# A fused two-block decoder on one core: conditioning weights partly summed ahead of their matmul, and causal attention outputs with the values stationary

## The reference, cut to what matters

```
sh1, sc1, g1, sh2, sc2, g2 = split(silu_c @ ada_w[i] + ada_b[i], 6)       # and the same with silu(c_ctx)
h = rmsnorm(x, norm_mix[i]) * (1.0 + sc1) + sh1
x = x + g1 * attention(h);  x = x + g2 * conv_ffn(rmsnorm(x, norm_ffn[i]) * (1.0 + sc2) + sh2)
```

```
o_nsa = g0 * o_cmp + g1 * softmax(causal(q @ k_s.T)) @ v_s + g2 * softmax(causal(q @ k_w.T)) @ v_w
o_fox = softmax(causal(f_q @ f_k.T + decay)) @ f_v                        # 4 heads of 64
o_pool, o_conv = moving averages, short causal convolution
for i, o in enumerate((o_nsa, o_pool, o_conv, o_fox)):
    acc += sigmoid(merge[i]) * ((o * silu(gates[i])) @ w_branch[i])
x = x + acc @ w_out
```

## Time and profile before

| | |
|---|---|
| median of three runs | 1595.04 us (1594.56 to 1595.25) |
| the profiled execution | 1595.22 us |
| its span (first to last instruction) | 1593.4 us |
| granted TensorE clock, mean | 0.997 |
| PE busy | 1568.6 us, 98% |
| DVE / ACT / POOL busy | 936.4 / 750.5 / 543.3 us |
| layer 0 of block two starts about | 1094 us; layer 1 is the same pattern some 255 us later |

### The profile page before, as it was taken

One profiled execution on the slowest core, in us unless ns is written; L12 is line 12 of the kernel. 1 busy time (PEld: TensorE's weight loads), 2 busy tenths in 40 slices (PEclk: granted clock), 3 DMA queues, 4 the chain that ended last, 5 costly groups with the idle time before them and its releaser, 6 DMA issues.

```text
span 1593.4 us, 23097 instructions
## 1 busy us (share of the span) xinstructions
PE 1568.6 (98%) x9146; PEld 1303.4 (82%) x9146; DVE 936.4 (59%) x1441; ACT 750.5 (47%) x1360; POOL 543.3 (34%) x354
## 2 busy tenths in 40 slices
PE   8999999999999999999999999999999999999998
PEld 5778557778887888879768899989998889998887
DVE  4434485555575554342266888757876457968435
ACT  5324485444322433243375755445654445654444
POOL 2224243322211222212273111007424657623663
PEclk9999999999999999999999999999999999999999
DMA  9264500534174222364313754454534534633551
GB/s 393 94 246 187 212 30 9 204 135 157 63 268 184 80 81 73 124 207 164 123 37 113 267 192 172 162 190 170 183 133 161 199 143 171 215 133 132 185 211 54
DMA packets 52603, 249.17 MB, mean 156 GB/s; under 512 B 20624, under 2 KB 21008, under 8 KB 26256
## 3 DMA queue, kind: packets, MB, share of 16 engines
q1 hardware_dynamic: 43744, 243.90, 42.2%
q10 hardware_dynamic: 8752, 3.80, 1.0%
HBM read 246.63 MB, written 1.05 MB: 155 GB/s over the span
## 4 chain that ended last, share of the span: by engine, by line
PE 88%; DVE 5%; ACT 3%; issue 1%; DMA 1%; POOL 1%; SPq 0%; POOLq 0%; ACTq 0%; DVEq 0%
PE psq L554 16%; PE psq L555 16%; PE psq L556 16%; PE ps L554 7%; PE ps L556 7%; PE ps L555 7%; PE psq L970 3%; PE ps L568 1%; PE psq L971 1%; PE ps L970 1%; DMA RAW<-wstream 1%; ACT WHL L526 1%; PE psq L1365 1%; PE ps L1393 1%; PE psq L2298 1%
## 5 line engine op out<-in xcount | busy, mean ns | idle before, releaser
L536 DVE TENSOR_TENSOR WHL<-RAW,WHL 128x1024 fp32r<-128x1024 f32 (+3 forms) x264 | 324.9, 1254 | 290.1 <-ACT WHL L526 289.6
L536 POOL TENSOR_TENSOR WHL<-RAW,WHL 128x1024 fp32r<-128x1024 f32 (+2 forms) x116 | 304.5, 2627 | 504.6 <-ACT WHL L526 471.8
L526 ACT ACTIVATE WHL<-RAW 128x1024 fp32r<-128x1024 f32 (+2 forms) x380 | 361.4, 1002 | 196.1 <-DMA RAW<-wstream 98.6
L554 PE MATMUL psq<-NHL,WHL 128*128 128x256 f32 (+1 forms) x1072 | 353.8, 330 | 1.7 <-POOL WHL L536 0.7
L555 PE MATMUL psq<-NHL,WHL 128*128 128x256 f32 (+1 forms) x1072 | 349.0, 326 | 0.0
L556 PE MATMUL psq<-NHL,WHL 128*128 128x256 f32 (+1 forms) x1072 | 348.9, 325 | 0.0
L554 PEld LDWEIGHTS psq<-NHL,WHL 128*128 128x128 f32 x1072 | 205.2, 191 | 28.9 <-issue 7.5
L556 PEld LDWEIGHTS psq<-NHL,WHL 128*128 128x128 f32 x1072 | 205.3, 191 | 16.6
L555 PEld LDWEIGHTS psq<-NHL,WHL 128*128 128x128 f32 x1072 | 205.3, 191 | 15.4
L554 PE MATMUL psq<-WHL,NHL 128*128 128x512 f32 (+1 forms) x320 | 124.8, 390 | 1.7 <-DVE WHL L536 1.7
L556 PE MATMUL psq<-WHL,NHL 128*128 128x512 f32 (+1 forms) x320 | 123.3, 385 | 0.0
(11 more groups left out here) (389 smaller groups left out, 2975.6 us busy)
## 6 DMA issues: line engine op xcount, KB each, us to landing
RAW<-wstream SPq DMA_DIRECT2D x194, 1024.0 KB, 4.8
RAW<-wstream SPq DMA_DIRECT2D x32, 704.0 KB, 4.0
K<-first SPq DMA_DIRECT2D x4, 1024.0 KB, 17.2
RAW<-wstream SPq DMA_DIRECT2D x4, 800.0 KB, 4.3
X<-xin SPq DMA_DIRECT2D x2, 1024.0 KB, 6.1
V<-first SPq DMA_DIRECT2D x2, 1024.0 KB, 19.3
Q<-first SPq DMA_DIRECT2D x2, 1024.0 KB, 24.7
BR<-rpb ACTq DMA_DIRECT2D x8, 256.0 KB, 8.2
```

What stands on the lines that cost most here:

```text
L526: e.activation(WH[:, u % 3, a:z], RAW[:, v % 3, a:z], ACT.Copy).then_inc(w_hi, 1)
L536: e.tensor_tensor(WL[:, u % 3, a:z], RAW[:, v % 3, a:z], WH[:, u % 3, a:z].bitcast(F32), ALU.subtract).then_inc(w_lo_p if pool else w_lo_v, 1)
L554: e.matmul(o, lh, rh, start=start, stop=False)
```

## The change

**Conditioning.** In pass b=1 units 0, 1, 6 and 7 are no longer multiplied on PE: DVE adds each of them, times a column of CB, into two buffers of 128x2048 (one for c, one for c_ctx), units 0 and 1 ahead of the splits of projection units 1 and 2, units 6 and 7 behind the whole rotation loop. Units 2 to 5 stay on PE, two after projection unit 5 and two after 6. A joint matmul of both sums (8 matmuls) stands ahead of value unit 1, the turn ahead of value unit 2. Pass b=3 has its units 4 to 7 summed at MLP units 1, 3, 5, 7 in the same way, with the joint ahead of unit 8. In passes 5 and 6 the units only run closer together. A load behind a summed unit now waits for DVE's sum.

**Hybrid layers.** DVE multiplies the probabilities by the reciprocal (times the gate) in SBUF, ahead of their transposes (`dve_causal_scale`, nine TENSOR_TENSORs of 128x512 per layer), and the transposes wait for that in place of the exponential. The output matmul holds 64 columns of values stationary in either half of the array's columns, with 128 or 256 columns of probabilities moving, so that outputs arrive transposed, all in one PSUM bank; the selected, the window and the compressed attention add up there. `dve_causal_out`, `dve_cmp_out` and the transposes `pe_turn_nsa` and `pe_turn_fox` are gone. Fox's output times its gate runs on DVE after scale 4, its high part on ACT after exponential 5, the rest on DVE after scale 5; output matmul 2 waits for the first of them, since it reuses the bank.

**Heads and g2.** A weight split moves into the norm loop, ACT's copy of KF moves behind a split, and the first half of g2's matmuls is put ahead of the scores of job 0.

```diff
-UP_ADA = {("up", 0, 0): (0, 1, 2, 3), ("up", 0, 2): (4,), ("up", 0, 3): (5,), ("up", 0, 4): (6,), ("up", 0, 5): (7,)}
-QKV_ADA = {("qkv", 1, 4): (0, 1, 2), ("qkv", 1, 5): (3,)}
-JOINT_ADA = {("up", 0, HALF_FT + 1): (7,)}
-LATE_ADA = {("up", 1, 0): (0, 1, 2), ("up", 1, 1): (3,)}
+FIRST_ADA = {3: (0,), 4: (1,), 5: (2, 3), 6: (4, 5), 9: (6,), 10: (7,)}
+FIRST_SUMMED = {1: (0,), 2: (1,)}
+FIRST_ON_PE = {5: (2, 3), 6: (4, 5)}
+UP_ADA = {("up", 0, 0): (0, 1, 2, 3)}
+UP_SUMMED = {1: 4, 3: 5, 5: 6, 7: 7}
+QKV_ADA = {("qkv", 1, 4): (0, 1, 2, 3)}
+LATE_ADA = {("up", 1, 0): (0, 1, 2, 3)}
+SUMMED = {1: (0, 1, 6, 7), 3: (4, 5, 6, 7), 4: tuple(range(8))}
+JOINT_AT = {("qkv", 0, 9): 1, ("up", 0, 8): 3, ("up", 0, HALF_FT + 1): 4}
...
-            if v >= 3 and KEYS[v - 3][:2] == ("ada", 4):
-                e.wait_ge(ada_acc, KEYS[v - 3][2] + 1)
+            if v >= 3 and KEYS[v - 3] in ADA_ACC:
+                e.wait_ge(ada_acc, ADA_ACC[KEYS[v - 3]])
...
-        def dve_ada_step(e, k):
-            v = UNIT_OF["ada", 4, k]
+        def weight_sums(b):
+            if b == 1:
+                return [t.rearrange("p a n -> p (a n)") for t in (PP[:, 3:7, :], TMP[:, 4:8, :])]
+            return [WSUM[:, c, :] for c in range(1 if b == 4 else 2)]
+
+        def dve_ada_step(e, b, k):
+            v = UNIT_OF["ada", b, k]
+            sums = weight_sums(b)
+            at = ADA_ACC["ada", b, k] - len(sums)
             e.wait_ge(d_raw[v % 3], 16 * (v // 3 + 1))
-            if k == 0:
-                e.tensor_scalar(WSUM[:, :], RAW[:, v % 3, :], CB[:, k, 0:1], None, ALU.mult).then_inc(ada_acc, 1)
-                return
-            e.wait_ge(ada_acc, k)
-            e.scalar_tensor_tensor(out=WSUM[:, :], in0=RAW[:, v % 3, :], scalar=CB[:, k, 0:1], in1=WSUM[:, :],
-                                   op0=ALU.mult, op1=ALU.add).then_inc(ada_acc, 1)
-
-        def pe_ada_joint(e):
-            e.wait_ge(ada_par, 3)
-            e.wait_ge(ada_acc, 8)
-            for j in range(4):
-                mm = e.matmul(AB[32 * j:32 * j + 32, :], ONE.to_broadcast([P, 32]), WSUM[:, 512 * j:512 * j + 512],
-                              start=True, stop=True)
+            if b == 4 and k == 0:
+                e.wait_ge(gemm, product(("joint", 3)))
+            for c, t in enumerate(sums):
+                if k == SUMMED[b][0]:
+                    e.tensor_scalar(t, RAW[:, v % 3, :], CB[:, k, c:c + 1], None, ALU.mult).then_inc(ada_acc, 1)
+                    continue
+                e.wait_ge(ada_acc, at - len(sums) + c + 1)
+                e.scalar_tensor_tensor(out=t, in0=RAW[:, v % 3, :], scalar=CB[:, k, c:c + 1], in1=t,
+                                       op0=ALU.mult, op1=ALU.add).then_inc(ada_acc, 1)
+
+        CBF = CB[:, :, :].rearrange("p k n -> p (k n)")
+        ONE_AT = (CBF[:, 16:48], CBF[:, 15:47])
+
+        def pe_ada_joint(e, b):
+            if b == 4:
+                e.wait_ge(ada_par, 3)
+            e.wait_ge(ada_acc, ADA_ACC["ada", b, SUMMED[b][-1]])
+            for c, t in enumerate(weight_sums(b)):
+                for j in range(4):
+                    mm = e.matmul(AB[32 * j:32 * j + 32, :], ONE_AT[c], t[:, 512 * j:512 * j + 512], start=b == 4,
+                                  stop=b == 4 or c == 1)
             mm.then_inc(gemm, 1)
 
         def act_ada_row(e, b):
-            e.wait_ge(gemm, product(("ada", b, ada_units(b) - 1)))
+            e.wait_ge(gemm, product(("joint", b) if b in SUMMED else ("ada", b, ada_units(b) - 1)))
...
-                    for _ in range((0, 0, 0, 2, 2, 2, 1, 1)[i]):
-                        pe_ada(e, 1, next(late_ada))
+                    for k in FIRST_ON_PE.get(i, ()):
+                        pe_ada(e, 1, k)
             for i in range(4):
                 if l == 0 and i == 1:
+                    pe_ada_joint(e, 1)
+                if l == 0 and i == 2:
                     pe_ada_turn(e, 1)
                 pe_values(e, l, i)
...
+                if l == 0:
+                    for k in FIRST_SUMMED.get(i, ()):
+                        dve_ada_step(e, 1, k)
...
-            dve_ada(e, 1 if l == 0 else 5)
+            if l == 0:
+                dve_ada_step(e, 1, 6)
+                dve_ada_step(e, 1, 7)
             for i in range(3):
+                if i == (1 if l == 0 else 0):
+                    dve_ada(e, 1 if l == 0 else 5)
                 split_lo(e, ahead(("qkv", l, 8 + i)), False)
...
+        def dve_causal_scale(e, l, i):
+
+            kind, qt, nk, g0 = causal_job(l, i)
+            r = STAT[:, i, 8:12].rearrange("p (l r) -> p r l", r=2)
+            e.wait_ge(att_r, r_done(l, i))
+            if qt == 0:
+                p = TMP[:, p_tiles(qt)[0], :].rearrange("p (r l k) -> p r l k", r=2, l=2)
+                e.tensor_tensor(p, p, r.unsqueeze(3).to_broadcast([P, 2, 2, P]), ALU.mult).then_inc(p_scaled, 1)
+                return
+            for g, tile in enumerate(p_tiles(qt)):
+                p = TMP[:, tile, :].rearrange("p (l k) -> p l k", l=2)
+                e.tensor_tensor(p, p, r[:, g, :].unsqueeze(2).to_broadcast([P, 2, 256]), ALU.mult).then_inc(p_scaled, 1)
+
...
-                e.wait_ge(att_exp, EXP_BASE + 24 * l + 4 * i + per * (g + 1))
+                e.wait_ge(p_scaled, g0 + g + 1)
...
         def pe_causal_pv(e, l, i):
             kind, qt, nk, g0 = causal_job(l, i)
-            per = 512 // nk
             e.wait_ge(att_pt, TR_BASE + 11 * l + tr_count(i + 1))
-            if i:
-                e.wait_ge(att_o, O_BASE + 8 * l + i)
             if i == 0:
                 e.wait_ge(sb_copy, copied(l, "v"))
-            o = bank[2][:, 256 * (i % 2):256 * (i % 2) + 256]
-            for n, h in enumerate(HEADS):
-                for k in range(qt + 1):
-                    c = ((n % per) * (qt + 1) + k) * P
-                    v = VF[:, k, 64 * h:64 * h + 64] if kind == 2 else VN[:, k, 64 * kind:64 * kind + 64]
-                    mm = e.matmul(o[:, 64 * h:64 * h + 64], TMP[:, t_tiles(qt)[n // per], c:c + P], v, start=k == 0,
-                                  stop=k == qt)
+            if i == 2:
+                e.wait_ge(z_mul, z_value(l, 3))
+            for k in range(qt + 1):
+                for a in range(2 if kind == 2 else 1):
+                    for par in range(2):
+                        half = slice(64 * par, 64 * par + 64)
+                        o = bank[2][half, :].rearrange("p (c q) -> p c q", c=2)[:, :, qt * P:qt * P + P]
+                        t = TMP[:, t_tiles(qt)[par if qt else 0], :].rearrange("p (n q) -> p n q", n=4)
+                        t = t[:, k:4:2, :] if qt else t[:, 2 * par:2 * par + 2, :]
+                        if kind == 2:
+                            v, o, t = VF[:, k, 128 * a + 64 * par:128 * a + 64 * par + 64], o[:, a, :], t[:, a, :]
+                        else:
+                            v = VN[:, k, 64 * kind:64 * kind + 64]
+                        mm = e.matmul(o, v, t, start=i in (0, 2) and k + a == 0, stop=kind == 2 and k == qt,
+                                      skip_group_check=True)
             mm.then_inc(att_pv, 1)
-
...
-        def pe_cmp_pv(e, l, qt):
-            e.wait_ge(att_pt, TR_BASE + 11 * l + 10 + qt)
-            e.matmul(bank[3 + qt][:, 0:256], TMP[:, 6, 128 * qt:128 * qt + P], VCB, start=True,
-                     stop=True).then_inc(att_pv, 1)
-
-        def dve_cmp_out(e, l, qt):
-            x = TMP[:, 8 + qt, 256:512]
-            g = GS[:, qt, 0:4].unsqueeze(2).to_broadcast([P, 4, 64])
-            e.wait_ge(att_pv, PV_BASE + 8 * l + 7 + qt)
-            e.wait_ge(gs_v, l + 1)
-            e.tensor_tensor(x.rearrange("p (h d) -> p h d", h=4),
-                            bank[3 + qt][:, 0:256].rearrange("p (h d) -> p h d", h=4), g, ALU.mult).then_inc(att_o, 1)
-            e.wait_ge(att_o, O_BASE + 8 * l + 6 + 2 * qt)
-            e.wait_ge(nsa_o, 4 * l + 2 * qt + 1)
-            e.tensor_tensor(ON[:, qt, :], ON[:, qt, :], x, ALU.add).then_inc(nsa_o, 1)
+        def pe_cmp_pv(e, l):
+            e.wait_ge(att_pt, TR_BASE + 11 * l + 11)
+            for c in range(2):
+                mm = e.matmul(bank[2][:, 256 * c:256 * c + 256], VCB[:, P * c:P * c + P], TMP[:, 6, 0:256], start=False,
+                              stop=True, skip_group_check=True)
+            mm.then_inc(att_pv, 1)
...
-        Z_ORDER = (1, 2, 0, 3)
+        Z_ORDER = (3, 1, 2, 0)
...
+        FOX_Z, NSA_Z = wide2(TMP[:, 8, :]), wide2(TMP[:, 7, :])
+
+        def dve_fox_gated(e, l):
+            e.wait_ge(att_pv, PV_BASE + 7 * l + 2)
+            dve_gated(e, l, 3, pair(bank[2]), FOX_Z)
+
+        def dve_nsa_gated(e, l):
+            e.wait_ge(att_pv, PV_BASE + 7 * l + 7)
+            dve_gated(e, l, 0, pair(bank[2]), NSA_Z)
...
             pe_compress_sum(e, l)
+            pe_proj(e, l, "g2", (0,))
             pe_causal_qk(e, l, 0)
-            pe_gates(e, l, 2)
+            pe_proj(e, l, "g2", (1,))
             pe_compress_down(e, l)
...
             dve_gates(e, l, 2)
```

(11 more changed lines are left out.)

180 lines of the change are left out of this document (73 added, 107 removed).

## The result

The changed kernel took 1623.57 us, median of four (1621.57 to 1627.83), against 1595.04 before: the ratio on record is 1.0183, with its 95% interval from 1.0162 to 1.0204 (the two medians alone give 1.0179). It is slower, clear of the noise and as forecast, but by 28.5 us and not by 18.4, and 1.6 us above the upper end of the range. The profiled execution took 1622.86 us.

A forecast was written before the change was run, and what follows sets the result against it. PE, 98% busy, was taken as the bound, with DVE and ACT's slackless mutual waiting ending beside it. 1595.2 + 8.5 - 1.0 - 2.1 - 0.6 + 11.2 (layers) + 2.2 (clock) = 1613.4 us; own range 1606 to 1622, overall 1587 to 1622.

The forecast's parts named there:

- the end of the rotation loop: Pass b=1, DVE: loop ends at 133.9 to 136.4 us, middle 135.2; four sums of 9.9 us follow.
- the joint's length in b=1: Pass b=1, PE: the joint matmul of the sums runs 1.9 us, then value unit 1 starts.
- the head of layer 0: Start of a hybrid layer: the moved weight split saves about 0.3 us.
- what PE wins back behind the merge: Layer 0 behind the merge: shorter outputs 4 and 5 and transposes save 2.0 us, an earlier start 0.3.
- the clock in the new pauses: PE's new pauses in the layers: half of three clock falls of 1.46 us, +2.2 us, bounds 0 to 4.4.
- the ring of DVE and ACT: Hybrid layers: DVE and ACT wait for each other in turn without slack, so any work added there is paid.
- Rival A: Whole kernel: nothing binds, DVE absorbs sums and scalings, all PE savings count: -16.1, 1579 us; chance 0.12.
- B: Whole kernel: the sums of b=1 hold PE, but the hybrid layers gain: 1588.6 us; chance 0.14.
- C: Whole kernel: layers bound as forecast, but sums of units 6 and 7 end in time: 1603.2 us; chance 0.16.
- Pass b=1: First projection: PE waits for DVE's sums ahead of the joint, +8.5 us, bounds -2.0 to +11.
- Absorption and the other passes: After b=1: two short waits shrink, -1.0 us; pass b=3 saves 2.1; passes 5 and 6 save 0.3 each.
- The ring of a layer: Hybrid layer up to the merge: scalings and fox's gating add +8.0 us, bounds +6.2 to +12.5.

The follow-up runs named there:

- the filler run: The changed kernel with seven matmuls of zeros filling PE's pause ahead of merge unit (0, 0): 1619.62 us, ratio 1.0152.

## Why the prediction was wrong in size

In short: what holds PE was told rightly, and five terms came out worse than forecast. These are the end of the rotation loop and the joint's length in b=1, the absorption behind it, the head of layer 0, what PE wins back behind the merge, and above all the clock in the new pauses.

**What bounds the kernel: right.** PE has no slack, and the ring of DVE and ACT ends with it. The run with the scalings on DVE is slower by 16.3 us, the one with them on POOL by nothing that can be measured, and the 2.3 us that the heads gave PE were worth nothing. Rival A (nothing binds) and B (the layers gain) fall with that; C (the sums of b=1 in time) falls with the run of the conditioning alone. The two main releasers were as named: L601 ahead of the joint, `dve_conv_u` ahead of the merge. Of the waits named for the layers, those ahead of output 2 and the merge came; those ahead of transposes 1 and 5 did not (0.7 us once, in layer 1).

**Pass b=1: mechanism right, +8.5 should have been +11.1.** The step put value unit 1 at 147.0; it came at 150.33. Three errors make this up. The loop's end was bounded by 133.9 and 136.4, with 135.2 taken, and the last sums began at 137.57: +2.4. The sums took 9.1 us (137.57 to 146.7), not 9.9: -0.8. And the joint was priced at 1.9 us, the price at full clock, and took 3.6: +1.7. These make 3.3; 0.35 of it goes because the step counted from the turn (138.86) and not from value unit 1 itself (139.21), and 0.4 because it had added as much for POOL. That the turn and the splits behind DVE's sums would add nothing was right.

The loop's end failed for a reason that the step had not seen. It took the last split to wait for ACT and the transfer. The transfer did come early, and ACT's part started 5.7 us sooner (127.13 against 132.81), but DVE had become the last to be ready: it works without a pause from 123.15 to 146.7 and reached that split at 133.88, only 0.3 us earlier. POOL's split moved forward with ACT's part, from 134.89 to 129.22, and held a rotation of the iteration before instead (2.65 us at 129.24). The last iteration itself, with no held operation, took 3.7 us in place of 6.4.

**Absorption and the other passes: too hopeful.** Behind value unit 1 the delay grew on to +11.7, and PE's two longest waits behind it, ahead of the units of b=2, did not shrink (0.69 and 0.86 us, before 0.69 and 0.83). Pass b=3 gave 2.9 (+11.7 to +8.8), 0.8 more than forecast. Pass 5 gave 0.6, and pass 6 lost 0.7 again: PE now waits 0.92 and 1.45 us for transfers at 888 and 891; its two longest waits in that stretch had been 0.82 and 0.29. Up to the first hybrid layer 4.8 was forecast and 8.9 came: 4.1 too little.

**The ring of a layer: right.** Forecast was +8.0 from the first maximum to the merge; it was 18.9 - 10.2 = 8.7 in layer 0, and 27.1 - 19.0 = 8.1 in layer 1, where 7.8 was forecast. Scaling 0 and 1 were held as told (2.09 and 2.40 us; forecast as delays of 1.1 and 2.6), and the others ran in 0.69 each. The outputs were priced right too: 3.0 us less a layer was forecast, and over both layers their busy time fell from 17.4 to 11.1. From layer start to merge the delay grew by 10.0 in layer 0, 2.0 more than forecast, of which 1.3 arose in the head; in layer 1 by 7.0, 0.8 less.

**The head: the step failed.** It was put at a gain of 0.3. The moved split alone gave more, 1.0 us in each layer (PE's wait of 0.83 at 1095.26 is gone). But PE waited 2.2 us for L548 in layer 0, the clock fell behind that wait, and 3.0 us were won when the copy of the keys stood back in its place. I had followed the moved instruction to who waits for it, but not to the order in which DVE and POOL then meet. The clock of g2 came back as told, 1.3 us of the 1.46, and was worth nothing ahead of a ring that did not move.

**Behind the merge: too much.** The step took -2.3; the delay fell by 1.2 in layer 0 and 1.6 in layer 1, 1.8 too little.

**The clock: right mechanism, under half the size.** The term was +2.2, half of three falls of 1.46 us, with 4.4 as its bound. The lower level stands at the joint (1.7 us), at both merges (2.3 and 2.2), behind the wait in the head, and twice behind the wait for the output of job 2, where the merge's wait hides it. What reaches the end is 1.7 + 2.3 + 2.2 = 6.2; for the 4.5 of the two merges the filler run measured 4.0. Both halves of the term failed: the price of a fall came from one stretch of small matmuls, and I took half, where each of the six new pauses (2.2, 3.0, 3.35, 3.41, 3.44 and 11.7 us) brought a fall.

**Together**, against the profiled execution, 27.6 measured and 18.2 forecast: 4.1 (up to the hybrid layers, the joint's clock in it) + 2.0 - 0.8 (to the merges) + 4.5 (clock at the merges) + 1.8 (behind them) - 2.2 (the clock term already in the sum) = 9.4. The upper end of the range, 1622, was too low because the head had no bound of its own, the loop's end came out above its bound, and the clock's bound of 4.4 lay below what came.

## What to carry to other kernels

Where two engines hand work to each other without slack, price an added operation by what this ring pays, and look first for an engine with nothing behind it: the same 18 products cost 15.5 us more on DVE than on POOL, though POOL needs 1.5 times as long for one. Where PE is the bound and a wait like these appears (3.4 us and 11.7 us here), add the fall of the clock behind it at once (1.7 to 2.3 us each), and see whether PE can ask one unit later: a joint that stood one unit too early cost 14.5 us. And a gain ahead of a stage that something else ends is worth nothing until that other thing moves, while moving the one operation that stood last (`dve_conv_u`) gave 10.4 us.

## What the runs showed of the hardware that I had not expected

- A wait of 1.18 us at the merge in the run with the heads alone was already followed by a stretch with a granted clock of 0.62; it stood behind a row of small matmuls. The wait of 0.77 us at the same place in layer 1 was not (1.00). In the kernel after, waits of 3.44, 3.35 and 11.72 us were followed by 0.50. After the fourteen small filler instructions, 3.20 us in place of a pause, the clock stayed at 1.00.
- DVE's and POOL's shares of one weight split (128x1024 each, all in SBUF) meet in the head of hybrid layer 0. With POOL 0.43 us ahead they took 2.72 us on POOL and 3.38 on DVE; with both starting at 1125.91 they took 1.21 on DVE and 3.45 on POOL. A shift of one ACT copy turned it round, and the kernel with the copy back in its place was 3.0 us faster.
- POOL multiplied 128x512 of SBUF by a broadcast factor in 1.04 us, against 0.69 on DVE.
